# Token halves between the two layers of a hybrid attention kernel, with GpSimd adding residuals and summing squares

## The chip, the cores and the metric

One Trainium2 chip, of which the kernel uses one core. The metric is the time of one execution on the device, in microseconds (us). A core has five engines that run from queues of their own and wait for each other by semaphores: TensorE (PE in the profile; PEld is its weight load), VectorE (DVE), ScalarE (ACT), GpSimd (POOL) and SyncE (SP), which here only issues DMAs.

## The reference

Two layers are computed one after the other on 512 tokens of width 2048, in float32: a first layer with latent attention (MLA) and forgetting attention, and a second one with compressed, selected and windowed attention. What matters here lies between them:

```python
def _hybrid_layer(x, ...):
    ...
    o = jnp.concatenate([o_mla, o_fox], axis=-1) @ w_out
    return x + _rms_norm(o, g_post)

def second_block(x, w_in, ...):
    h = _rmsnorm(x, norm_g[l])
    proj = h @ w_in[l]
```

So the output projection `o` of the first layer needs its norm over all 2048 features, is scaled and added to `x`, and the sum needs a norm of its own before the second layer's projection. The second norm's factor per token can be applied after the projection, the first one's can't, since `x` is added in between.

## The kernel before

Activations lie transposed: 128 features on the partitions, 512 tokens along a row, 16 such tiles (`KT`) for 2048 features, in the array `o`. Each float32 product is made of three matmuls (`three`, line 419): a high part of the weights with a high part and with a rest of the activations, and the rest of the weights with the high part. `xh` and `xl` hold the two parts of the activations, `wh` and `wl` those of the weights.

Weights come in units of 128 x 1024 into four slots. SyncE loads a unit into `raw` once the slot's unit before it has been split; ScalarE copies the high part into `wh` (`act_hi`, line 973, which waits until TensorE has used the slot, `w_used`), and VectorE subtracts to get `wl` (`lo`, line 1429). A strip is 128 output features: two units, 16 x 3 matmuls of 512 columns.

The output projection of the first layer (`U_OUT1`) is 16 strips (`half`, line 440). VectorE evacuates each (`out1`, line 1898), ScalarE squares it into `e_t`, and VectorE adds the squares into `acc`. After the last strip:

- TensorE sums the columns of `acc` and `e_t` (`pe_token_sums`, line 548), so that each token's sum of squares lies on a partition.
- VectorE and ScalarE make the factor per token and lay it on diagonal matrices in `gate` (`token_rms`, line 1535; `act_root`, line 1018), and TensorE spreads it over all partitions with a matmul (`pe_spread`, line 560), into the PSUM bank `po`.
- TensorE runs six filler matmuls (`WARM_MID`, line 714).
- VectorE scales each tile by `g_post` and that bank (`scale_tile`, line 1923). Tiles 0 and 1 get `x` added by VectorE from `xr1` (`residual`, line 1928). For tiles 2 to 15 GpSimd issues a DMA that adds `x` from memory into the tile (line 389), at most four in flight, and it stores the sums to memory in four DMAs (line 383) for the end of the second layer.
- ScalarE makes `xh` and the squares of each tile (lines 1258 and 1261), VectorE makes `xl` (`x_rest`, line 1594) and adds the squares to `acc` (`square_in`, line 1602).
- TensorE runs four strips of the second projection at once, tile by tile (`pe_four`, line 517): 16 x 4 x 3 matmuls of 512 columns, and ahead of its last two tiles the sum of squares of the second norm (`pe_sum`, line 543).

The order of the work is written out by hand, engine by engine, and each queue is executed in order. At the very end of the kernel the same work is already done in token halves (`last_strip`, line 929), where GpSimd multiplies five tiles per half (line 416), and that stage is used below as a source of durations. It starts at about 1815 us.

## Time and profile before

| | us |
|---|---|
| median of 3 runs | 1853.12 |
| lowest and highest run | 1852.43, 1853.68 |
| the profiled execution, its own time | 1853.12 |
| its span, first to last instruction | 1851.4 |
| PE busy | 1823.4 (98%) |
| VectorE, ScalarE, GpSimd busy | 1047.4, 665.6, 36.3 |
| mean granted clock of TensorE | 0.994 of full speed |

The profile is of one execution. A line of it names an engine, a source line, what was written and from what, a count and times. Matmuls are pipelined, so the distance between the starts of two of them tells their cost, not the length of one record. On the other engines, too, an instruction can start a little before the end of the record before it. A row of the chain of waits is a start, a length and the engine and line on which the end of the kernel depended at that time.

### The profile page before, as it was taken

How to read it: one execution, taken by the hardware profiler on the slowest of the kernel's cores; microseconds unless marked ns; L12 is line 12 of the kernel's file. 1: busy time of each engine (PE TensorE's matmuls, PEld its weight loads, DVE VectorE, ACT ScalarE, POOL GpSimd, SP SyncE). 2: the span in 40 equal slices, each digit the busy share in tenths (PEclk: the TensorE clock that was granted, in tenths of full speed). 3: DMA queues.
4: the chain of work that ended last, by engine and by line, in shares of the span. 5: the costliest groups of instructions: out<-in, count | busy, mean ns of one | idle time of the engine just before them, and what ended most of it. 6: DMA issues, size and time to landing. Idle time of an engine off the chain costs nothing.

```text
span 1851.4 us, 25537 instructions
## 1 busy us (share of the span) xinstructions
PE 1823.4 (98%) x9060; PEld 1514.8 (82%) x9060; DVE 1047.4 (57%) x1768; ACT 665.6 (36%) x1279; POOL 36.3 (2%) x58
## 2 busy tenths in 40 slices
PE   9999999999999999999999999999999999999997
PEld 7788888888888887878868887888888888888887
DVE  7643434444433787853348954766767566665334
ACT  6532332322223544432226342433433333443222
POOL 0000000000000000000002000000000000000001
PEclk9999999999999999999999999999999999999998
DMA  6322222222232333232237363211112222124333
GB/s 237 106 86 91 79 79 91 86 84 82 89 102 80 126 114 113 91 112 93 91 101 218 102 227 124 70 57 57 68 57 69 92 68 79 66 70 136 115 115 102
DMA packets 56021, 186.16 MB, mean 101 GB/s; under 512 B 6688, under 2 KB 11168, under 8 KB 55456
## 3 DMA queue, kind: packets, MB, share of 16 engines
q1 hardware_dynamic: 51328, 170.78, 27.6%
q0 software_dynamic: 4640, 14.68, 3.0%
q8 instruction: 33, 0.54, 0.1%
q14 instruction: 20, 0.16, 0.0%
HBM read 177.05 MB, written 8.39 MB: 100 GB/s over the span
## 4 chain that ended last, share of the span: by engine, by line
PE 90%; DVE 5%; DVEq 2%; ACT 1%; issue 1%; POOL 0%; POOLq 0%; ACTq 0%
PE strip L421 23%; PE strip L423 22%; PE strip L422 22%; PE scores L421 4%; PE scores L422 3%; PE scores L423 3%; PE outputs L423 2%; PE outputs L422 2%; PE outputs L421 1%; PE scores L476 1%; PE scores L869 1%; PE scores L828 1%; PE scores L897 1%; DVE wl L1433 1%; DVEq L1438 0%
## 5 line engine op out<-in xcount | busy, mean ns | idle before, releaser
L421 PE MATMUL strip<-xh,wh 128*128 128x512 f32 (+1 forms) x1976 | 779.7, 395 | 5.7 <-DVE xl L1825 3.2
L423 PE MATMUL strip<-xh,wl 128*128 128x512 f32 (+1 forms) x1976 | 768.0, 389 | 0.0
L422 PE MATMUL strip<-xl,wh 128*128 128x512 f32 (+1 forms) x1976 | 767.2, 388 | 0.0
L421 PEld LDWEIGHTS strip<-xh,wh 128*128 128x128 f32 x1976 | 371.9, 188 | 82.4 <-DVE xl L1825 4.8
L423 PEld LDWEIGHTS strip<-xh,wl 128*128 128x128 f32 x1976 | 371.6, 188 | 77.3
L422 PEld LDWEIGHTS strip<-xl,wh 128*128 128x128 f32 x1976 | 372.3, 188 | 72.7 <-issue 0.7
L1433 DVE TENSOR_TENSOR wl<-raw,wh 128x1024 fp32r<-128x1024 f32 (+3 forms) x306 | 354.7, 1177 | 119.1 <-ACT wh L979 118.2
L979 ACT ACTIVATE wh<-raw 128x1024 fp32r<-128x1024 f32 (+3 forms) x308 | 306.9, 1023 | 109.7 <-PE strip L423 107.1
L1001 ACT ACTIVATE prob<-scores,nms 128x128 f32<-128x128 f32 (+3 forms) x128 | 65.9, 532 | 129.7 <-DVE nms L1481 129.7
L1241 ACT ACTIVATE e_t<-o 128x512 f32 (+1 forms) x30 | 19.0, 632 | 222.0 <-DVE o L1902 118.1
L421 PE MATMUL scores<-xh,wh 128*128 128x512 f32 (+1 forms) x240 | 91.6, 382 | 0.0
L423 PE MATMUL scores<-xh,wl 128*128 128x512 f32 (+1 forms) x240 | 90.1, 375 | 0.0
L422 PE MATMUL scores<-xl,wh 128*128 128x512 f32 (+1 forms) x240 | 90.0, 375 | 0.0
L1441 DVE TENSOR_TENSOR y<-strip,rb 128x512 f32<-128x512 f32 x45 | 31.1, 692 | 75.7 <-PE strip L423 73.1
L1479 DVE TENSOR_REDUCE nm<-scores 128x1 f32<-128x128 f32 (+1 forms) x96 | 41.2, 485 | 55.1 <-PE scores L457 54.3
L984 ACT ACTIVATE q_h<-y 128x512 fp32r<-128x512 f32 x24 | 15.2, 632 | 145.8 <-DVE y L1454 107.2
L994 ACT ACTIVATE e_t<-y 128x512 f32<-128x512 f32 x32 | 20.5, 641 | 127.4 <-DVE y L1441 127.4
L1505 DVE TENSOR_TENSOR ptl<-scores,pth 128x512 fp32r<-128x512 f32 (+3 forms) x128 | 53.8, 483 | 9.7 <-ACT pth L1009 9.6
L421 PEld LDWEIGHTS scores<-xh,wh 128*128 128x128 f32 x240 | 45.2, 188 | 9.0 <-issue 0.5
L422 PEld LDWEIGHTS scores<-xl,wh 128*128 128x128 f32 x240 | 45.2, 188 | 8.7 <-issue 0.7
L423 PEld LDWEIGHTS scores<-xh,wl 128*128 128x128 f32 x240 | 45.2, 188 | 8.1
L1902 DVE COPY o<-strip 128x512 f32 (+1 forms) x14 | 9.7, 692 | 74.0 <-PE strip L423 73.9
(426 smaller groups left out, 1875.6 us busy)
## 6 DMA issues: line engine op xcount, KB each, us to landing
raw<-in_w SPq DMA_DIRECT2D x308, 512.0 KB, 3.2
xn<-o POOLq DMA_DIRECT2D x4, 1024.0 KB, 7.8
xr<-xn POOLq DMA_DIRECT2D x16, 256.0 KB, 3.0
o<-in_xt SPq DMA_DIRECT2D x7, 512.0 KB, 7.9
o<-in_xt POOLq DMA_DIRECT2D x14, 256.0 KB, 6.3
out<-o SPq DMA_DIRECT2D x14, 256.0 KB, 2.7
raw<-in_w SPq DMA_DIRECT2D x2, 256.0 KB, 4.6
o<-in_xt SPq DMA_DIRECT2D x2, 256.0 KB, 5.1
```

What stands on the lines that cost most here:

```text
L421: pe.matmul(out, ah, bh, start=first, stop=False, skip_group_check=shared)
L422: pe.matmul(out, ah, bl, start=False, stop=False, skip_group_check=shared)
L423: return pe.matmul(out, al, bh, start=False, stop=last, skip_group_check=shared)
L476: ins = pe.transpose(sb[t][:, P * (w - t):P * (w - t) + P], prob[:, ROW[w] + P * t:ROW[w] + P * t + P], ident[:, :])
L979: a.activation(wh[s][:, :cols], raw[s][:, :cols], ACT.Copy).then_inc(w_hi, 1)
L994: a.activation(e_t[:, :], src, ACT.Tanh, scale=0.5).then_inc(ev_act, 1)
L1001: a.activation(prob[:, ROW[t]:ROW[t] + w], sb[t][:, pre[t]:pre[t] + w], ACT.Exp, bias=nms[:, t:t + 1], scale=scale, accum_out=lsum[:, t:t ...
L1241: a.activation(e_t[:, :], src, ACT.Square).then_inc(ev_act, 1)
L1433: v_.tensor_tensor(wl[s][:, :cols], raw[s][:, :cols], wh[s][:, :cols].bitcast(F32), ALU.subtract)\
L1441: v_.tensor_tensor(dst, src[:, :], times[:, :], ALU.mult).then_inc(y_done, 1)
L1479: v_.tensor_reduce(nm[:, t:t + 1], sb[t][:, 0:P * (t + 1)], AX.X, ALU.max, negate=True)
L1505: v_.tensor_tensor(ptl[:, cols], sb[t][:, 0:w], pth[:, cols].bitcast(F32), ALU.subtract)\
```

## The change

The last two strips of the first layer and the first six tiles (`HT = 6`) of the second projection are worked in two halves of 256 tokens. The sums, the factor and the spreading are done once for each half. GpSimd adds `x` to tiles 0 to 5 from `xr1`, which now holds six tiles and lies elsewhere in memory, half by half, and sums all squares of the second norm into a new array `acc_mid`; four buffers `sq` take the place of two. The additions into `acc_mid` wait for each other by the semaphore `sq_used`, with no drain between them. Tiles 6 to 15 still get `x` by accumulating DMAs. The filler matmuls are gone. Semaphore counts that the end of the kernel waits for are moved along; its work is the same.

The diff, cut to its core:

```diff
-WARM_FIRST, WARM_MID = 5, 6
+WARM_FIRST = 5
+HT = 6
+X_MID = 3 * KT - 6
+X_OUT2 = 4 * KT - 6 + HT
...
-    sq = [place("sq0", [P, S], offset=at["prob"] + 2048), place("sq1", [P, S], offset=at["prob"] + 4096)]
+    sq = [place("sq0", [P, S], offset=at["prob"] + 2048), place("sq1", [P, S], offset=at["prob"] + 4096),
+          place("sq2", [P, S], offset=at["pth"] + 2048), place("sq3", [P, S], offset=at["pth"] + 4096)]
+    acc_mid = place("acc_mid", [P, S], offset=at["pth"])
...
-    xr1 = place("xr1", [P, 2, S], offset=at["y"])
...
+    xr1 = place("xr1", [P, HT, S], offset=kv0)
...
+    def sq_part(hf, j):
+        n_ = HT * hf + j
+        return sq[n_ // 2 % 4][:, 256 * (n_ % 2):256 * (n_ % 2) + 256]
...
+        g.memset(acc_mid[:, :], 0.0).then_inc(blk_zero, 1)
+        g.dma_start(xr1[:, :, :], d["xt"][:, 0:HT, :]).then_inc(xr1_in, 16)
         g.dma_start(cos2[:, :], d["cos_a"]).then_inc(tab2_in, 16)
         g.dma_start(sin2[:, :], d["sin_a"]).then_inc(tab2_in, 16)
+        def residual(hf, j):
+            g.wait_ge(scaled, HT * hf + j + 1)
+            part = o[:, j, TOKENS[hf]]
+            g.tensor_tensor(part, part, xr1[:, j, TOKENS[hf]], ALU.add).then_inc(xn_done, 1)
...
+        def x_added_in(j):
+            if j - 4 >= HT:
+                x_is_added(j - 4)
+            g.wait_ge(scaled, HT + j + 1)
+            g.dma_start(o[:, j, :], d["xt"][:, j, :], accum_op=ALU.add).then_inc(x_added[j % 4], 16)
+        def square_half(hf, j):
+            if HT * hf + j:
+                g.wait_ge(sq_used, KT + HT * hf + j)
+            else:
+                g.wait_ge(blk_zero, 2)
+            g.wait_ge(sq_done, KT + HT * hf + j + 1)
+            g.tensor_tensor(acc_mid[:, TOKENS[hf]], acc_mid[:, TOKENS[hf]], sq_part(hf, j), ALU.add).then_inc(sq_used, 1)
+        def square(j):
+            g.wait_ge(sq_used, KT + HT + j)
+            g.wait_ge(sq_done, KT + HT + j + 1)
+            g.tensor_tensor(acc_mid[:, :], acc_mid[:, :], sq[j % 4][:, :], ALU.add).then_inc(sq_used, 1)
...
-        for j in range(2, KT):
-            if j >= 6:
-                x_is_added(j - 4)
-            g.wait_ge(scaled, j - 1)
-            g.dma_start(o[:, j, :], d["xt"][:, j, :], accum_op=ALU.add).then_inc(x_added[j % 4], 16)
-            if j == 7:
-                g.wait_ge(xn_done, 2)
-            if j in (7, 11, 15):
-                xn_store(j - 7)
+        g.wait_ge(xr1_in, 16)
+        for j in range(HT):
+            residual(0, j)
+            if j >= 3:
+                square_half(0, j - 3)
+        residual(1, 0)
+        square_half(0, 3)
+        residual(1, 1)
+        square_half(0, 4)
+        residual(1, 2)
+        x_added_in(6)
+        residual(1, 3)
+        x_added_in(7)
+        residual(1, 4)
+        square_half(0, 5)
+        residual(1, 5)
+        x_added_in(8)
+        square_half(1, 0)
+        x_added_in(9)
+        for j in range(1, HT):
+            square_half(1, j)
+        g.wait_ge(xn_done, 2 * HT)
+        xn_store(0)
+        for j in range(HT, KT):
+            if j + 4 < KT:
+                x_added_in(j + 4)
+            if j == 8:
+                xn_store(4)
+            if j == 12:
+                xn_store(8)
+            square(j)
...
+    def pe_mid(pe, u0, outs, aside):
+        def tile(j, s, tokens, first, last):
+            slot = (u0 + j // 2) % SLOTS
+            cols = slice(512 * (j % 2) + P * s, 512 * (j % 2) + P * s + P)
+            return three(pe, outs[s][:, tokens], wh[slot][:, cols], wl[slot][:, cols], xh[:, j, tokens],
+                         xl[:, j, tokens], first, last, shared=True)
+        for hf in range(2):
+            for j in range(HT):
+                pe.wait_ge(x_lo, X_MID + HT * hf + j + 1)
+                if hf == 0 and j % 2 == 0:
+                    pe.wait_ge(w_lo, u0 + j // 2 + 1)
+                for s in range(4):
+                    ins = tile(j, s, TOKENS[hf], hf == 0 and j == 0, False)
+                if hf == 1 and j % 2 == 1:
+                    ins.then_inc(w_used, 1)
+                if hf == 0:
+                    aside(j)
+        for u in range(HT // 2, 8):
+            if u == 7:
+                pe.wait_ge(sq_used, KT + HT + KT)
+                pe.matmul(px[:, :], ones[:, :], acc_mid[:, :], start=True, stop=True).then_inc(sum_done, 1)
+            steps = [(2 * u + a, s) for a in range(2) for s in range(4)]
+            if u == 7:
+                steps = [(2 * u + a, s) for s in range(4) for a in range(2)]
+            for j, s in steps:
+                if s == 0:
+                    pe.wait_ge(x_lo, X_MID + HT + j + 1)
+                    pe.wait_ge(w_lo, u0 + u + 1)
+                ins = tile(j, s, slice(0, S), False, j == KT - 1)
+                if j == KT - 1 and s < 3:
+                    ins.then_inc(four_done, 1)
+            ins.then_inc(w_used, 1)
...
-        pe_token_sums(pe, 3, N_OUT1 + KT)
-        pe_spread(pe, 0, (po,))
-        for i in range(WARM_MID):
-            pe.matmul(px[:, :], ones[:, :], gate[:, :], start=True, stop=True)
-        pe_four(pe, U_CMPIN, 3 * KT - 6, sb, summed=(4, 7))
+        def out1_half(hf, j, steps):
+            if steps[0] == 0:
+                if hf == 0:
+                    pe.wait_ge(y_done, N_OUT1 + 13 + j)
+                else:
+                    pe.wait_ge(half_out, j + 1)
+            pe_half_strip(pe, U_CMPIN - 4 + 2 * j, pj[(N_OUT1 + j) % 2], hf, steps)
+        out1_half(0, 0, range(KT))
+        out1_half(0, 1, range(KT))
+        out1_half(1, 0, range(5))
+        pe_half_sums(pe, 0, 4, (half_sq, 2))
+        out1_half(1, 0, range(5, KT))
+        pe.wait_ge(diag_done, 2)
+        pe.matmul(po[:, 0:256], ones[:, :], gate[:, 0:256], start=True, stop=True).then_inc(spread, 1)
+        out1_half(1, 1, range(KT))
+        def aside(j):
+            if j == 1:
+                pe_half_sums(pe, 1, 5, (ev_act, N_OUT1 + KT))
+            if j == 3:
+                pe.wait_ge(diag_done, NQ)
+                pe.matmul(px[:, :], ones[:, :], gate[:, :], start=True, stop=True).then_inc(spread, 1)
+        pe_mid(pe, U_CMPIN, sb, aside)
...
+        def sq_half(hf, j):
+            if HT * hf + j >= 8:
+                a.wait_ge(sq_used, KT + HT * hf + j - 7)
+            a.activation(sq_part(hf, j), o[:, j, TOKENS[hf]], ACT.Square).then_inc(sq_done, 1)
+        half_square(0, 0)
+        half_square(0, 1)
+        act_root(a, 3, 0, 2)
+        half_square(1, 0)
+        act_hi(a, At(U_CMPIN))
+        xh_half(0, 0)
+        xh_half(0, 1)
+        act_hi(a, At(U_CMPIN + 1))
+        xh_half(0, 2)
+        for j in range(3):
+            sq_half(0, j)
+        xh_half(0, 3)
+        half_square(1, 1)
         act_hi(a, At(U_CMPIN + 2))
+        xh_half(0, 4)
+        sq_half(0, 3)
+        xh_half(0, 5)
+        act_root(a, 4, 2, 4)
         act_hi(a, At(U_CMPIN + 3))
-        act_root(a, 3)
-        for j in range(KT):
-            if j < 2:
-                a.wait_ge(xn_done, j + 1)
-            else:
-                a.wait_ge(x_added[j % 4], 16 * (j // 4 + (j % 4 >= 2)))
+        for j in (4, 5):
+            sq_half(0, j)
+        for j in range(HT):
+            xh_half(1, j)
+            if j in (3, 5):
+                act_hi(a, At(U_CMPIN + (j + 5) // 2))
+            sq_half(1, j)
+        for j in range(HT, KT):
+            a.wait_ge(x_added[j % 4], 16 * ((j - HT) // 4 + 1))
             a.activation(xh[:, j, :], o[:, j, :], ACT.Copy, scale=c("g_2", j)).then_inc(x_hi, 1)
-            if j >= 2:
-                a.wait_ge(sq_used, KT + j - 1)
-            a.activation(sq[j % 2][:, :], o[:, j, :], ACT.Square).then_inc(sq_done, 1)
-            if j in (5, 7, 9, 11):
-                act_hi(a, At(U_CMPIN + (j + 3) // 2))
+            a.wait_ge(sq_used, KT + 2 * j - 6 if j < 9 else KT + HT + j - 3)
+            a.activation(sq[j % 4][:, :], o[:, j, :], ACT.Square).then_inc(sq_done, 1)
+            if j in (8, 10):
+                act_hi(a, At(U_CMPIN + j // 2 + 2))
         act_hi(a, At(U_CMPIN + 8))
-        act_rms(a, 4)
+        act_rms(a, 5)
...
+        def out1_half(hf, j):
+            if hf == 0:
+                v_.wait_ge(part_done, j + 1)
+            else:
+                v_.wait_ge(w_used, U_CMPIN - 2 + 2 * j)
+            v_.tensor_copy(o[:, 14 + j, TOKENS[hf]], pj[(N_OUT1 + j) % 2][:, 0:256])\
+              .then_inc(half_out if hf == 0 else y_done, 1)
+        def half_add(hf):
+            v_.drain()
+            if hf == 0:
+                v_.wait_ge(half_sq, 1)
+            else:
+                v_.wait_ge(ev_act, N_OUT1 + 15)
+            v_.tensor_tensor(acc[:, TOKENS[hf]], acc[:, TOKENS[hf]], e_t[:, TOKENS[hf]], ALU.add)
+            v_.drain().then_inc(acc_ready, 1)
+        def scale_half(hf, j):
+            factor = (po[:, 0:256], px[:, 256:512])[hf]
+            v_.scalar_tensor_tensor(o[:, j, TOKENS[hf]], o[:, j, TOKENS[hf]], c("g_post", j), factor, ALU.mult, ALU.mult)\
+              .then_inc(scaled, 1)
+        def rest_half(hf, j):
+            v_.wait_ge(x_hi, X_MID + HT * hf + j + 1)
+            v_.scalar_tensor_tensor(xl[:, j, TOKENS[hf]], o[:, j, TOKENS[hf]], c("g_2", j),
+                                    xh[:, j, TOKENS[hf]].bitcast(F32), ALU.mult, ALU.subtract).then_inc(x_lo, 1)
+        def scale_tile(j):
+            v_.scalar_tensor_tensor(o[:, j, :], o[:, j, :], c("g_post", j), px[:, :], ALU.mult, ALU.mult).then_inc(scaled, 1)
         for j in range(2):
             out1(0, 0)(j, U_OUT1 + 3 + j)
         two_strips(At(U_OUT1 + 4), out1(2, 0, banks=sb[0:2]))
         with v_.Fori(1, KT // 2 - 2) as i:
             two_strips(At(U_OUT1 + 4, i, 4), out1(2, i))
-        two_strips(At(U_CMPIN - 4), out1(14, 0, True))
-        token_rms(v_, 3)
-        v_.memset(acc[:, :], 0.0)
+        for j in range(2):
+            lo(v_, At(U_CMPIN - 2 + j))
+        out1_half(0, 0)
+        half_add(0)
+        out1_half(0, 1)
+        token_rms(v_, 3, 0, 2)
+        out1_half(1, 0)
+        v_.wait_ge(spread, 1)
+        scale_half(0, 0)
+        scale_half(0, 1)
+        half_add(1)
+        v_.drain().then_inc(r_done, 1)
+        scale_half(0, 2)
+        lo(v_, At(U_CMPIN))
+        rest_half(0, 0)
+        rest_half(0, 1)
+        scale_half(0, 3)
+        lo(v_, At(U_CMPIN + 1))
+        rest_half(0, 2)
+        out1_half(1, 1)
+        v_.drain().then_inc(r_done, 1)
+        scale_half(0, 4)
+        scale_half(0, 5)
+        rest_half(0, 3)
         lo(v_, At(U_CMPIN + 2))
+        rest_half(0, 4)
+        token_rms(v_, 4, 2, 4)
+        rest_half(0, 5)
         lo(v_, At(U_CMPIN + 3))
-        v_.wait_ge(spread, 1)
-        def scale_tile(j):
-            ins = v_.scalar_tensor_tensor(o[:, j, :], o[:, j, :], c("g_post", j), po[:, :], ALU.mult, ALU.mult)
-            if j >= 2:
-                ins.then_inc(scaled, 1)
-        def residual(j):
-            v_.drain()
-            v_.tensor_tensor(o[:, j, :], o[:, j, :], xr1[:, j, :], ALU.add).then_inc(xn_done, 1)
-        scale_tile(0)
-        v_.wait_ge(xr1_in, 16)
-        residual(0)
-        scale_tile(2)
-        scale_tile(1)
-        x_rest(0, o[:, 0, :], c("g_2", 0), 3 * KT - 6)
-        residual(1)
-        scale_tile(3)
-        for j in range(KT):
+        v_.wait_ge(spread, 2)
+        for j in range(3):
+            scale_half(1, j)
+        rest_half(1, 0)
+        scale_half(1, 3)
+        rest_half(1, 1)
+        scale_half(1, 4)
+        rest_half(1, 2)
+        scale_half(1, 5)
+        scale_tile(6)
+        rest_half(1, 3)
+        scale_tile(7)
+        rest_half(1, 4)
+        rest_half(1, 5)
+        lo(v_, At(U_CMPIN + 4))
+        scale_tile(8)
+        scale_tile(9)
+        for j in range(HT, KT):
+            x_rest(j, o[:, j, :], c("g_2", j), X_MID + HT)
             if j + 4 < KT:
                 scale_tile(j + 4)
-            if j:
-                x_rest(j, o[:, j, :], c("g_2", j), 3 * KT - 6)
-            if j:
-                square_in(j - 1, KT)
-            if j in (5, 7, 9, 11):
-                lo(v_, At(U_CMPIN + (j + 3) // 2))
-        square_in(KT - 1, KT)
-        v_.drain().then_inc(acc_ready, 1)
+            if j in (6, 8, 10):
+                lo(v_, At(U_CMPIN + j // 2 + 2))
         lo(v_, At(U_CMPIN + 8))
-        rms_ms(v_, 4, D)
-        rms_rb(v_, 4, rb)
+        rms_ms(v_, 5, D)
+        rms_rb(v_, 5, rb)
```

## Rows read from the trace of the kernel before

**Rows 1.** The page: busy time of each engine
```profile
PE 1823.4 (98%) x9060; PEld 1514.8 (82%) x9060; DVE 1047.4 (57%) x1768; ACT 665.6 (36%) x1279; POOL 36.3 (2%) x58
```

**Rows 2.** Chain of waits, 955 to 970 us (start, us, what)
```profile
955.37 0.24 PE strip L423
...
961.01 2.07 PE outputs L564 x2
963.08 6.84 PE odds L715 x12
969.92 0.23 PE scores L421
```

**Rows 3.** Busy time by stretch: engines, granted clock, DMA share, GB/s
```profile
963.00:967.00 4.00, 4.00 (x7) 1.64 (x6) 3.93 (x6) 1.24 (x2) 0.90 (x1) 0.58 0.69 211
```

**Rows 4.** The timeline of PE: weight strips, 512 columns (start, us, what)
```profile
949.99 0.39 PE L421 MATMUL strip<-xh,wh 128*128 128x512 f32 x1
950.22 0.39 PE L422 MATMUL strip<-xl,wh 128*128 128x512 f32 x1
```

**Rows 5.** The timeline of PE in the last stage: 256 columns and column sums
```profile
1820.07 0.28 PE L422 MATMUL strip<-xl,wh 128*128 128x256 f32 x1
1820.19 0.28 PE L423 MATMUL strip<-xh,wl 128*128 128x256 f32 x1
...
1827.15 0.50 PE L948 MATMUL odds<-ones,acc 128*128 128x1 f32 x4
...
1827.96 0.36 PE L421 MATMUL scores<-xh,wh 128*128 128x256 f32 x1
```

**Rows 6.** The chain of waits, the sum of squares at 1008 us
```profile
1008.04 0.86 PE odds L546 x2
```

**Rows 7.** The timeline of VectorE in the last stage
```profile
1821.42 0.43 DVE L2257 TENSOR_TENSOR acc<-acc,e_t 128x256 f32<-128x256 f32 x1 [2.22 <-ACT e_t L1423]
...
1828.13 0.16 DVE L1539 TENSOR_SCALAR nm<-odds 128x2 f32<-128x2 f32 x1 [3.17 <-PE odds L952]
...
1829.52 0.48 DVE L1550 TENSOR_SCALAR gate<-ident,rinv 128x128 f32<-128x128 f32 x2
...
1832.27 0.83 DVE L2257 TENSOR_TENSOR acc<-acc,e_t 128x256 f32<-128x256 f32 x1 [0.73 <-ACT e_t L1423]
1833.23 4.40 DVE L2242 SCALAR_TENSOR_TENSOR o<-o,cvec,outputs 128x256 f32<-128x256 f32 x11
```

**Rows 8.** The timeline of GpSimd in the last stage; one addition, two, then five
```profile
1832.08 0.73 POOL L416 TENSOR_TENSOR o<-o,rb 128x256 f32<-128x256 f32 x1 [17.06 <-ACT rb L1426]
...
1832.78 0.91 POOL L416 TENSOR_TENSOR o<-o,rb 128x256 f32<-128x256 f32 x1
...
1843.60 3.45 POOL L416 TENSOR_TENSOR o<-o,rb 128x256 f32<-128x256 f32 x5 [7.82 <-ACT rb L1426]
```

**Rows 9.** Groups of VectorE, 955 to 1006 us (busy us, mean ns, idle before)
```profile
L1599 DVE SCALAR_TENSOR_TENSOR xl<-o,cvec,xh 128x512 fp32r<-128x512 f32 x16 | 12.0, 747 | 0.3 <-ACT xh L1258 0.3
L1924 DVE SCALAR_TENSOR_TENSOR o<-o,cvec,outputs 128x512 f32<-128x512 f32 x16 | 11.6, 742 | 0.0
...
L1433 DVE TENSOR_TENSOR wl<-raw,wh 128x1024 fp32r<-128x1024 f32 x7 | 8.4, 1212 | 0.1
```

**Rows 10.** ScalarE, 256-column squares: durations ns min/median/max, first and last start
```profile
L1423 ACT ACTIVATE e_t<-o x4: 401/412/419, 1821.0 to 1838.0; 128x256 f32<-128x256 f32 x4
```

**Rows 11.** GpSimd: two DMA issues; length and landing of the accumulating ones
```profile
974.61 0.87 POOL L389 DMA_DIRECT2D o<-in_xt  x1 [1.24 <-DVE o L1924]
975.15 0.89 POOL L383 DMA_DIRECT2D xn<-o  x1
...
DMA to landing us min/median/max: 4.2/6.3/8.9
```

**Rows 12.** Line 416, GpSimd: durations ns min/median/max, first and last start
```profile
L416 POOL TENSOR_TENSOR o<-o,rb x10: 722/730/914, 1832.1 to 1846.3; 128x256 f32<-128x256 f32 x10
L416 POOLq MODIFY_POOL_CONFIG  x2: 37/37/37, 1815.0 to 1815.0; - x2
```

97 lines of the change are left out of this document (53 added, 44 removed).

## The prediction

> **What bounds the kernel now.** I read the page first, for what fills the span: TensorE (PE) is busy 98% of 1851.4 us, the others far less [rows 1]. So a change is worth only what it does to TensorE's stream. I then followed the chain of waits to where that stream carries no work of the reference. Between the layers the last weight strip's matmul ends at 955.61 (955.37 + 0.24), and the first matmul of the second layer's projection stands at 969.92 [rows 2]. The 14.3 us between them hold the column sums, the wait for the rms, the spreading matmul and 12 records of filler matmuls (6.84 us), which keep the clock up while VectorE, ScalarE and a DMA prepare the first tile. The granted clock fell all the same: 0.58 in 963 to 967 us, which is the lower level, 1.2 GHz [rows 3]. From 969.92 on TensorE stays dense.
>
> **The gap goes, and what TensorE does instead.** Strips 14 and 15 are cut into two token halves, so the rms, the scaling and the first projection tiles of tokens 0 to 255 are prepared while tokens 256 to 511 are still being multiplied.
> - Removed: 14.3 us.
> - Halves are dearer: a 512-column matmul comes every 0.227 us [rows 4], a 256-column one every 0.120 us, not 0.1134 [rows 5]. The change issues 192 of them for the strips and 2 x 6 x 4 x 3 = 144 for the first six projection tiles: 336 x 0.0066 = 2.2 us.
> - Column sums twice, 0.81 us each (1827.15 to 1827.96) [rows 5]: 1.6. Spreads: one of 512 columns at the 0.86 us of the sum of squares [rows 6], one of 256 at half of that: 1.3. The sum of squares at 1008 us stays.
>
> Net without a single wait: 14.3 - 2.2 - 1.6 - 1.3 = 9.2 us gained. Nearly all of it hangs on the helpers keeping up.
>
> **The helpers' durations.** VectorE, 256 columns with the factor in PSUM: 11 in 4.40 us, 0.40 apart, 0.475 long; an addition from SBUF 0.43; nm to the gate tiles 1828.13 to 1830.00, 1.87 [rows 7]. GpSimd, 256 columns: 0.73 alone, five in 3.45, so 0.68 to 0.70 apart [rows 8]. A 512-column addition on GpSimd is in no row: at least 0.73, at most two halves, 1.46; I take 1.30, nearer the upper end, since its fixed part is paid once. The rest tiles take 0.75, scaling 512 columns 0.74, the low part of a weight unit 1.21 [rows 9]. ScalarE needs 0.41 for 256 columns [rows 10]; its copy with a scale I take at 0.5. GpSimd issues two DMAs 0.54 apart, each 0.87 long, and an accumulating one lands after 4.2 to 8.9 us [rows 11]; an addition behind an issue starts 0.54 to 0.87 after it. A chained addition waits for the one before to end: 0.73 + 0.1 instead of 0.70; only the squares are chained, and the 10 late ones matter, 1 us in all, inside the 1.30 to 1.46. The configuration for GpSimd's additions ran at 1815.0, 17 us ahead of its first addition and unseen by it [rows 12]; now it comes with the early DMAs near 803 us: nothing.
>
> **Stretch A, up to the second spread.** The half strips start at 933.8 (955.6 less two strips of 10.9). 192 x 0.12 + 0.8 + 0.4 puts the first projection tile at 958.1, and four half tiles of 1.44 and the second column sums put TensorE at the second spread at 964.7. VectorE has, from the first spread at 952.5: 6 scalings (2.4), one addition (0.5), 3 weight lows at 1.14 apart (3.4), 5 half rests (2.0), a copy (0.4), the rms (1.9), 0.5 of waits: 963.6. Hidden, with 1 us of cover. Weight slots come free as each half-1 strip passes, 2 us ahead.
>
> **Stretch B, half 1 of tiles 0 to 5, and tile 6.** From the spread to the first rest: scale 0.5, GpSimd 0.9, ScalarE 0.55, rest 0.5, about as long as the two half tiles TensorE still has. Then GpSimd's written order bites. It issues the accumulating DMA of tile 6 ahead of the residual of tile 3, and that DMA waits for the scaling of tile 6, which VectorE does behind the rest of tile 2. From residual 2 to residual 3: 0.73 + 0.05 + 0.5 + 0.05 + 0.4 + 0.4 + 0.74 + 0.15 + 0.54 = 3.6 us, where TensorE eats a half tile in 1.44. Tile 7's DMA does the same ahead of residual 4: 3.2. Tile 6's own rest stands behind a weight low and two scalings (2.5). With 0.4 us of slack: stalls of 1.8, 1.7 and 1.7, together 5.2 us.
>
> **Stretch C, tiles 7 to 15.** TensorE wants the sum of squares 21.8 us after it starts tile 6 (8 x 2.72). GpSimd by then has 5 chained half squares (4.0), 10 full ones (13.0) and 11 DMA issues (5.9 to 9.6): 22.9 to 26.6. The last square comes about 1 us late, and tiles 8 and 10, whose data land late, cost 1.2: 2.2 us.
>
> So far: 9.2 - 5.2 - 2.2 = 1.8 us gained.
>
> **The new collision.** One place of the trace shows GpSimd adding beside a VectorE instruction that reads two SBUF tensors. The addition of line 2257 took 0.43 us at 1821.42, alone, and 0.83 at 1832.27, where GpSimd's addition had begun at 1832.08 [rows 7]. GpSimd's next one, 1832.78, took 0.91 where the others take 0.73 [rows 8]. So each waited for the other: 0.40 us on VectorE, 0.18 on GpSimd, though in 1843.60 to 1847.05, where VectorE's second operand lies in PSUM, five additions ran freely. This is one meeting, but the change makes dozens: 24 half and 10 full additions on GpSimd against 22 rests, 9 weight lows and one addition on VectorE, all reading two SBUF tensors.
> - A: about 6 meetings x 0.40 on VectorE = 2.4, less 1 of cover: TensorE waits 1.4 at the second spread.
> - B: each link of the chain is longer by a meeting; 1.3 more.
> - C: GpSimd has no slack left, and 10 squares of double width are each held up by a rest or a low, 2 x 0.18 = 0.36 each: 3.6 more. Upper issue spacing: 0.9 more.
>
> The Trainium skill (SBUF — State Buffer, "SBUF: two separate sides") states this as a rule: a VectorE instruction with two SBUF inputs and a reading GpSimd instruction exclude each other, the later one fully blocked. The trace agrees in kind, but not in full: blocked to the end of GpSimd's 0.73 us, the addition would have ended at 1833.24, and it ended at 1833.10. The same skill's GPSIMD Engine Reference (§3.1) gives about 2.6 cycles an element at 1.2 GHz, an estimate of 1.28 us for the unseen 512-column addition; the sum by it is the same.
>
> **Sum.** 1.8 - 1.4 - 1.3 - 3.6 - 0.9 = -5.4 us: slower. The profiled execution took 1853.12, equal to the median of the runs, for a span of 1851.4; so 1858.5 us. Bounds of this case: meetings at half their price and the lower issue spacing, 2.4 slower; additions of 1.46, landings of 6.8 and the higher prices, 9.9 slower: 1855.5 to 1863.0.
>
> **Rivals.** About 0.2%, 3.7 us, is what a measurement of this kernel can tell from no change.
> - Full exclusion: every meeting serial, GpSimd's 30 us of additions and VectorE's 24 us of two-input work in one line from 953 us. That is 54 us, so the last square ends at 1007 at best and, with the idle turns between, near 1013 to 1018; the projection ends 10 us later than now: 1863. For it the 0.40 us; against it that GpSimd lost only 0.18. The rule of the Trainium skill named above is this case.
> - No collision to speak of: the one meeting was an accident of dispatch. Then 1.8 gained, -1 to +4 by landing time: 1851.3.
> - Faster: GpSimd's order costs nothing because the scalings run ahead of my count, the stalls of B and C are under 3 us in all, and the gap's 9.2 us are kept to two thirds: 1847. It decides at tile 3 of half 1: if its rest is done within 1.5 us of tile 2's, this is the case. For it: VectorE and ScalarE have idle time between those tiles by my count. Against: the DMA of tile 6 stands ahead in GpSimd's queue whatever they do.
>
> **Chances.** The forecast 0.55 (0.42 slower by over 0.2%, 0.13 within), full exclusion 0.12 (slower), no collision 0.18 (0.13 within, 0.05 faster), stalls hidden 0.15 (faster). Faster 0.20, same 0.26, slower 0.54. The range 1850.5 to 1864.0 leaves out most of the last rival and the far end of full exclusion. The likeliest case's own range is 1855.5 to 1863.0.
>
> **What would show it.** No filler and no gap near 955; first projection tile 24 us after the half strips start; the second spread 1 to 2 us late; waits of TensorE on rest tiles 3, 4 and 6, each released by VectorE behind ScalarE behind GpSimd; VectorE's half rests at 0.8 to 1.0 us where they meet an addition, GpSimd's halves at 0.9 and more; the sum of squares waiting for GpSimd. Wrong if the rests keep 0.43 us beside GpSimd's additions, if a 512-column addition is far from 1.3 us, or if TensorE stands idle long enough for its clock to fall to the lower level, which would add to the loss.

## The result, and the profile after

The changed kernel takes 1864.87 us (median of 4 runs, 1863.67 to 1865.09), the kernel before 1853.40 (4 runs beside it): a ratio of 1.0061, 95% interval 1.0049 to 1.0073. It is slower, by 11.5 us (0.6%, and the interval leaves out no change), where 5.4 were forecast and 1864.0 was the end of the range.

First the page of the kernel after, to set against [rows 1]: its span, and busy time by engine.

```profile
span 1863.4 us, 25891 instructions
PE 1824.2 (98%) x9218; PEld 1522.3 (82%) x9218; DVE 1049.9 (56%) x1769; ACT 668.2 (36%) x1294; POOL 70.7 (4%) x89
```

TensorE (PE) is busy about as long as before, in a span 12.0 us longer: what is new is idle time. GpSimd (POOL) has gone from 36.3 us to 70.7. Next, what TensorE waited for between 930 and 1040 us: the timeline of the matmuls behind its waits (start, us, operation, and in brackets the idle time before it and what ended it). Two waits of 0.24 and 0.27, at tiles 7 and 9, are left out.

```profile
967.41 1.12 PE L836 MATMUL odds<-gate,ones 128*128 128x512 f32 x2 [1.31 <-DVE gate L1704]
978.62 0.39 PE L477 MATMUL scores<-xh,wh 128*128 128x256 f32 x1 [2.41 <-DVE xl L2084]
982.87 0.38 PE L477 MATMUL scores<-xh,wh 128*128 128x256 f32 x1 [2.55 <-DVE xl L2084]
987.92 0.51 PE L477 MATMUL scores<-xh,wh 128*128 128x512 f32 x1 [0.78 <-DVE xl L1753]
...
1004.33 0.50 PE L477 MATMUL scores<-xh,wh 128*128 128x512 f32 x1 [4.07 <-DVE xl L1753]
1019.11 1.12 PE L652 MATMUL odds<-acc_mid,ones 128*128 128x512 f32 x2 [2.00 <-POOL acc_mid L414]
```

The gap of [rows 2] is gone. In its place stand waits at the second spread (stretch A), at tiles 3 and 4 of the second half and at tile 6 (B), at tile 10 and at the sum of squares (C). Windows of after, with the columns of [rows 3] (the granted clock stands third from the end):

```profile
985.00:990.00 5.00, 4.22 (x20) 3.57 (x19) 5.00 (x6) 1.70 (x3) 4.25 (x5) 0.72 0.79 177
1000.00:1005.00 5.00, 0.93 (x5) 0.59 (x4) 1.42 (x3) 2.23 (x4) 3.59 (x4) 0.99 1.06 232
1005.00:1010.00 5.00, 5.00 (x17) 3.92 (x16) 4.54 (x4) 2.85 (x5) 2.76 (x3) 0.67 1.05 295
```

So the granted clock, too, falls twice, behind the waits of tile 4 and of tile 10; the means of 0.72 and 0.67 mix full speed with the lower level, 1.2 GHz. Now GpSimd, whose timeline answers to [rows 8] and [rows 11] (L401 and L417 issue DMAs, L392 adds a residual half, L409 half squares, L414 full ones):

```profile
975.83 0.92 POOL L401 DMA_DIRECT2D o<-in_xt  x1 [2.42 <-DVE o L2088]
976.44 1.06 POOL L392 TENSOR_TENSOR o<-o,xr 128x256 f32<-128x256 f32 x1
979.53 0.90 POOL L401 DMA_DIRECT2D o<-in_xt  x1 [2.02 <-DVE o L2088]
980.15 1.03 POOL L392 TENSOR_TENSOR o<-o,xr 128x256 f32<-128x256 f32 x1
...
987.57 6.33 POOL L409 TENSOR_TENSOR acc_mid<-acc_mid,sq 128x256 f32<-128x256 f32 x5
993.83 0.60 POOL L417 DMA_DIRECT2D xn<-o  x1
994.43 0.89 POOL L401 DMA_DIRECT2D o<-in_xt  x1
995.00 1.63 POOL L414 TENSOR_TENSOR acc_mid<-acc_mid,sq 128x512 f32<-128x512 f32 x1
...
1005.48 0.87 POOL L401 DMA_DIRECT2D o<-in_xt  x1 [1.89 <-DVE o L2088]
...
1009.42 0.86 POOL L401 DMA_DIRECT2D o<-in_xt  x1 [1.76 <-DVE o L2088]
```

Twice, at 975.83 and 979.53, a DMA issue waits for a scaling on VectorE with a residual behind it: stretch B as forecast. Then five half squares run in a row, and the DMA of tile 10 comes behind them and behind a store of 1 MB, at 994.43, although VectorE had finished that tile's scaling (L2088) at 988.5 by its own timeline. The transfer then took 8.3 us to land, where the middle of the ten took 5.4. First the scaling, then the landing of all ten and of tile 10's alone:

```profile
987.79 0.73 DVE L2088 SCALAR_TENSOR_TENSOR o<-o,cvec,odds 128x512 f32<-128x512 f32 x1
...
DMA to landing us min/median/max: 4.3/5.4/8.7
...
DMA to landing us min/median/max: 8.3/8.3/8.3
```

Last the groups of both engines in 935 to 1030 us (count, busy us, mean ns, idle before), for [rows 8, 9].

```profile
L414 POOL TENSOR_TENSOR acc_mid<-acc_mid,sq 128x512 f32<-128x512 f32 x10 | 17.7, 1770 | 0.2
L409 POOL TENSOR_TENSOR acc_mid<-acc_mid,sq 128x256 f32<-128x256 f32 x12 | 12.3, 1024 | 0.3
L1753 DVE SCALAR_TENSOR_TENSOR xl<-o,cvec,xh 128x512 fp32r<-128x512 f32 x10 | 14.8, 1490 | 6.7 <-ACT xh L1413 6.7
```

A full rest tile on VectorE takes 1.49 us on average, where it took 0.75.

**A measure for the runs.** The stage goes from the first half strip (934.96 in after; 933.8 in before by the forecast's working) to the first strip matmul behind the projection (1025.54; 1014.22). I split its length by windows into TensorE's idle time, its busy time times (1 - granted clock), and the rest; the split is good to some 0.2 us. The stages are of single profiled executions, and the times beside them medians of the timed runs, so a stage and a median do not always move alike: the profiled executions of order_a and set_after were the slowest of theirs (1861.65 and 1862.90), those of vsq and vsq2 the fastest (1849.55 and 1849.41).

| kernel | stage us | idle | lower clock | rest | time, ratio to before (95%) |
|---|---|---|---|---|---|
| before | 80.4 | 3.6 | 2.7 | 74.1 | 1853.40 |
| after | 90.6 | 13.6 | 3.2 | 73.8 | 1864.87, 1.0061 (1.0049 to 1.0073) |
| order_a | 86.8 | 10.3 | 3.2 | 73.3 | 1858.73, 1.0028 (1.0018 to 1.0039) |
| order_b | 88.3 | 11.3 | 3.7 | 73.4 | 1859.86, 1.0038 (1.0024 to 1.0053) |
| x10_first | 83.4 | 6.9 | 3.4 | 73.0 | 1855.91, 1.0011 (1.0001 to 1.0020) |
| store_late | 83.7 | 8.6 | 1.7 | 73.5 | 1857.43, 1.0023 (1.0012 to 1.0034) |
| no_sq | 79.5 | 5.0 | 1.7 | 72.9 | 1854.67, 1.0009 (0.9999 to 1.0018) |
| set_after | 88.6 | 9.9 | 5.5 | 73.2 | 1861.74, 1.0040 (1.0026 to 1.0053) |
| fill | 90.5 | 10.0 | 0.0 | 80.5 | 1865.61, 1.0064 (1.0050 to 1.0078) |
| vsq | 78.7 | 4.8 | 0.0 | 73.9 | 1851.72, 0.9988 (0.9979 to 0.9997) |
| vsq2 | 77.9 | 4.0 | 0.0 | 73.9 | 1850.23, 0.9984 (0.9975 to 0.9993) |

The stage holds 10.2 of the 12.0 us between the two spans. Another 0.7 lie behind it, and 1.1 before it: both kernels wait some 2.3 us for VectorE at 770 us, in code the change does not touch, and behind it the clock was at the lower level in the profiled execution of after and not in that of before. It was down there in 8 of the 16 profiles of this study other than micro's, so I take this for chance and no part of the change. First before, then after:

```profile
773.00:775.00 2.00, 2.00 (x9) 1.61 (x10) 1.83 (x6) 2.00 (x4) 0.00 (x0) 1.00 0.00 0
```

```profile
773.00:775.00 2.00, 2.00 (x6) 1.61 (x5) 1.83 (x7) 2.00 (x4) 0.00 (x0) 0.50 0.00 0
```

### The profile page after: what moved, and what is told of

It is laid out like the page before. It is cut to its first block, busy times and chain, and to the rows that moved or that the text cites. A ratio compares the mean times of both kernels' runs of the same rounds, so it can differ in the third digit from the quotient of the medians.

```text
span 1863.4 us, 25891 instructions
## 1 busy us (share of the span) xinstructions
PE 1824.2 (98%) x9218; PEld 1522.3 (82%) x9218; DVE 1049.9 (56%) x1769; ACT 668.2 (36%) x1294; POOL 70.7 (4%) x89
## 4 chain that ended last, share of the span: by engine, by line
PE 85%; DVE 6%; POOL 2%; issue 2%; DVEq 2%; ACT 2%; DMA 0%; POOLq 0%; ACTq 0%
PE strip L477 22%; PE strip L479 22%; PE strip L478 22%; PE scores L477 3%; PE scores L478 3%; PE scores L479 3%; PE outputs L479 2%; PE outputs L478 2%; PE outputs L477 1%; PE scores L532 1%; DVE wl L1587 1%; PE scores L991 1%; PE scores L950 1%; PE scores L1019 1%; POOL acc_mid L409 1%
## 5 line engine op out<-in xcount | busy, mean ns | idle before, releaser
L477 PEld LDWEIGHTS strip<-xh,wh 128*128 128x128 f32 x2008 | 378.2, 188 | 81.7 <-DVE xl L1979 4.8
L479 PEld LDWEIGHTS strip<-xh,wl 128*128 128x128 f32 x2008 | 378.1, 188 | 76.8
L478 PEld LDWEIGHTS strip<-xl,wh 128*128 128x128 f32 x2008 | 378.4, 188 | 72.0 <-issue 0.7
L477 PE MATMUL scores<-xh,wh 128*128 128x512 f32 (+1 forms) x264 | 97.8, 370 | 10.3 <-DVE xl L1753 5.4
L478 PEld LDWEIGHTS scores<-xl,wh 128*128 128x128 f32 x264 | 50.8, 192 | 7.6 <-issue 0.5
L479 PEld LDWEIGHTS scores<-xh,wl 128*128 128x128 f32 x264 | 50.7, 192 | 7.5
L1123 ACT ACTIVATE pth<-scores 128x512 fp32r<-128x512 f32 (+3 forms) x128 | 45.0, 437 | 12.3 <-PE scores L950 9.7
```

The costliest lines, as they stand in the source:

```text
L477: pe.matmul(out, ah, bh, start=first, stop=False, skip_group_check=shared)
L478: pe.matmul(out, ah, bl, start=False, stop=False, skip_group_check=shared)
L479: return pe.matmul(out, al, bh, start=False, stop=last, skip_group_check=shared)
L1123: a.activation(pth[:, COL[t]:COL[t] + w], sb[t][:, 0:w], ACT.Copy).then_inc(pt_hi, 1)
```

## Experiments

**The durations by themselves.** A small kernel with sections parted by barriers: `v.tensor_tensor` x12 and `g.tensor_tensor` x6, alone and side by side.

> The disputed durations by themselves. This kernel leaves out the whole computation and writes zeros; its sections, parted by barriers, hold 12 VectorE instructions of 512 columns and 6 GpSimd ones, first each alone, then side by side. Theory 1 (the collision is a property of two SBUF inputs on VectorE beside any GpSimd addition): alone VectorE 0.75 us, GpSimd 0.73 for 256 columns and 1.3 to 1.6 for 512; side by side each VectorE instruction that meets an addition takes 0.4 us and more longer, and GpSimd's 0.2; with VectorE's second operand in PSUM, and beside GpSimd's memset, nothing changes. Rival (GpSimd's 512-column addition is simply that slow, 1.6 us, and chaining adds 0.2): GpSimd 1.56 alone and 1.79 apart when chained alone, and little changes side by side. Full exclusion: side by side the two engines' times add up, 12 x 0.67 + 6 x 1.4 or more = 16 us and over for the section, against some 9 for the longer engine alone.

The timeline of its sections (start, us, what, count). Alone: VectorE 512 columns, GpSimd 256, 512, and 512 chained by a semaphore. Then side by side: 512 on both, and 512 with VectorE's second operand in PSUM; last VectorE beside memsets and beside accumulating DMAs.

```profile
6.42 7.32 DVE L65 TENSOR_TENSOR vout<-vin 128x512 f32<-128x512 f32 x12 [2.35 <-POOLq L105]
13.85 4.12 POOL L110 TENSOR_TENSOR gout<-gin 128x256 f32<-128x256 f32 x6 [12.16 <-DVEq L60]
18.14 7.35 POOL L113 TENSOR_TENSOR gout<-gin 128x512 f32<-128x512 f32 x6 [0.18 <-DVEq L60]
...
26.25 7.96 POOL L118 TENSOR_TENSOR gacc<-gacc,gin 128x512 f32<-128x512 f32 x6
34.32 13.71 DVE L75 TENSOR_TENSOR vout<-vin 128x512 f32<-128x512 f32 x12 [20.59 <-POOLq L105]
34.41 10.06 POOL L122 TENSOR_TENSOR gout<-gin 128x512 f32<-128x512 f32 x6 [0.20 <-POOL gacc L118]
...
55.58 7.26 DVE L83 TENSOR_TENSOR vout<-vin,bank 128x512 f32<-128x512 f32 x12
...
76.89 7.32 DVE L91 TENSOR_TENSOR vout<-vin 128x512 f32<-128x512 f32 x12
84.33 7.32 DVE L95 TENSOR_TENSOR vout<-vin 128x512 f32<-128x512 f32 x12
```

A 512-column addition comes every 0.61 us on VectorE (7.32 / 12), and on GpSimd every 1.22 us alone (7.35 / 6) and 1.33 chained (7.96 / 6). Side by side VectorE loses 13.71 - 7.32 = 6.4 us to six additions, 1.07 for each of 1.22, and GpSimd loses 0.45 for each. That is close to full exclusion: six of VectorE's instructions (3.7 us) and all of GpSimd's (7.35) fit into 10.06 us. In this small kernel it takes two SBUF inputs on VectorE and an addition, which reads SBUF, on GpSimd: with VectorE's second operand in PSUM, or a memset or accumulating DMAs on GpSimd's side, VectorE keeps 7.3. The rule of the Trainium skill (SBUF — State Buffer, "SBUF: two separate sides") says the same, that the later instruction fully blocks and that a GpSimd instruction which only writes does not count; this run agrees, but for 0.15 us of each addition.

**GpSimd's order in stretch B.** The residuals ahead of the DMAs.

```
         residual(1, 2)
-        x_added_in(6)
         residual(1, 3)
-        x_added_in(7)
         residual(1, 4)
-        square_half(0, 5)
         residual(1, 5)
+        x_added_in(6)
+        x_added_in(7)
+        square_half(0, 5)
         x_added_in(8)
```

> Only GpSimd's written order is changed, by putting the residuals of tiles 3 to 5 of the second half ahead of the accumulating DMAs of tiles 6 and 7. Queue-order theory: the waits of 2.41, 2.55 and 0.78 us before tiles 3 to 5 and the clock's fall behind them (1.1) go, and nothing inherits them: 6 us less than after, 1859. Rival (the squares are the bound of stretch C): tile 10's transfer stays behind GpSimd's burst of half squares, TensorE comes to it earlier and waits longer, 4 us becomes 8 or more: 1863 to 1865, same as after. In between if part of the wait is passed on.

The median fell by 6.1 us, to 1858.73; the stage of the profiled execution, the slowest of its eight, is 3.8 us shorter. All waits of TensorE in the stage:

```profile
967.60 1.12 PE L836 MATMUL odds<-gate,ones 128*128 128x512 f32 x2 [1.33 <-DVE gate L1704]
983.47 0.50 PE L477 MATMUL scores<-xh,wh 128*128 128x512 f32 x1 [2.58 <-DVE xl L1753]
1000.73 0.50 PE L477 MATMUL scores<-xh,wh 128*128 128x512 f32 x1 [4.45 <-DVE xl L1753]
1015.52 1.12 PE L652 MATMUL odds<-acc_mid,ones 128*128 128x512 f32 x2 [1.97 <-POOL acc_mid L414]
```

The waits of tiles 3 and 4 are gone (the one of 0.78 was tile 6's, not tile 5's as I had written). Tile 6's wait has grown to 2.58, so the expectation that nothing inherits them failed. Tile 10 and the sum wait about as before: the rival, that C takes the gain back, is out.

**And in stretch C.** On top of order_a, the DMAs of tiles 10 to 12 between the half squares, the later ones ahead of full squares, the stores later (their lines are left out here).

```
         square_half(1, 2)
+        x_added_in(10)
...
         square_half(1, 4)
+        x_added_in(11)
         square_half(1, 5)
+        x_added_in(12)
         for j in range(HT, KT):
-            if j + 4 < KT:
-                x_added_in(j + 4)
+            if j + 7 < KT:
+                x_added_in(j + 7)
```

> As order_a, and the accumulating DMAs of tiles 10 to 12 stand between the half squares, the stores of the normalised input come three tiles later. If order on GpSimd's queue is all that cost the time: no wait over 1 us on tiles 3 to 15, the sum of squares 1 to 2 us late, 1855 to 1857. If GpSimd's load (its additions 1.3 to 2.0 us long beside VectorE) is the bound: the tiles come in time but the sum of squares comes 4 us late and more, 1858 to 1860. If collisions alone set it, no order helps: 1863 and more.

1859.86, so neither: tile 10 no longer waits and tile 11 only 0.60, but the wait before the sum rose to 6.68. I took that for GpSimd's load. It was in good part again an order: tiles 13 to 15 have their issues ahead of squares that were ready (half_v, below, shows it). Moving tile 10's DMA alone, on top of order_a:

```
         x_added_in(9)
-        for j in range(1, HT):
+        square_half(1, 1)
+        square_half(1, 2)
+        x_added_in(10)
+        for j in range(3, HT):
             square_half(1, j)
...
-            if j + 4 < KT:
+            if HT < j and j + 4 < KT:
                 x_added_in(j + 4)
```

> The kernel order_a (whole computation) with the accumulating DMA of tile 10 alone put ahead of GpSimd's last three half squares; the store of 1 MB stays where it was. If the half squares ahead of the issue make tile 10 late: it is issued some 3.5 us earlier, the wait of 4.45 us before it falls to 1.5 or less; what of it comes back at the sum of squares (1.97 in order_a) tells how far GpSimd's load binds: all of it back, 1858.5; none, 1855.5. If the store beside it makes it late, the wait stays over 3 us.

1855.91, 2.8 us under order_a. Tile 10 does not wait any more, tile 11, whose DMA still stands behind the half squares, does; and the wait before the sum fell with them:

```profile
1001.64 0.57 PE L480 MATMUL scores<-xh,wh 128*128 128x512 f32 x1 [2.76 <-DVE xl L1756]
1011.96 1.12 PE L655 MATMUL odds<-acc_mid,ones 128*128 128x512 f32 x2 [0.26 <-POOL acc_mid L414]
```

So GpSimd was not the bound by its load: it had been waiting for VectorE, which waited for a transfer that GpSimd had issued late. But the move also took tile 10's DMA out from behind the store, so it does not part the two. The store's part, also on top of order_a:

```
-        g.wait_ge(xn_done, 2 * HT)
-        xn_store(0)
         for j in range(HT, KT):
             if j + 4 < KT:
                 x_added_in(j + 4)
             if j == 8:
+                g.wait_ge(xn_done, 2 * HT)
+                xn_store(0)
+            if j == 11:
                 xn_store(4)
-            if j == 12:
+            if j == 13:
                 xn_store(8)
```

> The kernel order_a (whole computation) with the 1 MB store of tiles 0 to 3 moved from ahead of tile 10's DMA to behind the issue for tile 12, and the next two stores moved later with it. If the store's traffic makes tile 10's transfer land late (8.3 us in after, median 5.4): the wait of 4.45 us before tile 10 falls by 2 to 3 us. If the half squares ahead of the issue do it: it falls by the 0.5 us of the issue at most, 1858 to 1859, as order_a.

Tile 10 now waits 0.83 instead of 4.45, more than the 2 to 3 us that the expectation gave the store's traffic. Its DMA was issued at 987.37, 54.1 us into the stage, where order_a had 54.7: hardly earlier. But it landed in half the time. Its landing in order_a, in store_late and in x10_first, where it also stands ahead of the store:

```profile
DMA to landing us min/median/max: 9.3/9.3/9.3
...
DMA to landing us min/median/max: 4.5/4.5/4.5
...
DMA to landing us min/median/max: 6.9/6.9/6.9
```

So the store beside the transfer makes tile 10 late as much as the squares ahead of it do, and either move alone takes most of the wait away. What is gained there is in part lost again: tile 11 waits 1.37 and the sum 2.44 (1.97 in order_a), and now the stores run beside the last transfers, one of which took 9.2 us. The stage is 83.7 us, as long as x10_first's 83.4; the time is 1857.43, 1.3 under order_a, with intervals that overlap.

**The squares, left out.** The sum of squares is a constant in this kernel, so it does not compute the result.

```
-            if j >= 3:
-                square_half(0, j - 3)
...
-            square(j)
...
-                pe.wait_ge(sq_used, KT + HT + KT)
+                pe.wait_ge(sq_done, KT + HT + KT)
```

> GpSimd's written order as in after, but its 22 additions of squares are left out (the sum of squares of the second norm is a constant instead, so this part of the computation is missing); residuals, DMAs and stores stay. What the squares cost beside everything else: if the squares and their meetings with VectorE hold the loss, tile 10's wait (4.1), the wait at the sum (2.0), the second spread's wait (1.3) and the clock's second fall (1.8) go, and only the waits of tiles 3 to 5 with their fall stay: 1855 to 1857. If the order is at fault alone: the waits of tiles 3 to 5 stay, and tile 10 goes too, 1857 to 1859. If neither, 1863.

1854.67: the squares on GpSimd as a whole cost 10.2 of after's 11.5 us. Tiles 3 and 4 still wait, 1.19 and 1.98, by the order of residuals and DMAs, with the residuals' own meetings still in it.

**The squares, without their reads.** Each addition replaced by chained memsets, first in order_b, then in after; the sum is again a constant. The edit for a full square:

```
-            g.tensor_tensor(acc_mid[:, :], acc_mid[:, :], sq[j % 4][:, :], ALU.add).then_inc(sq_used, 1)
+            for i in range(2):
+                g.memset(acc_mid[:, 256 * i:512], 16.0).then_inc(setm, 1)
+                g.wait_ge(setm, sets + i + 1)
+            g.memset(acc_mid[:, :], 16.0).then_inc(sq_used, 1)
```

> The kernel order_b with each of GpSimd's additions of squares replaced by chained memsets of about the length that such an addition has alone (three of 256 and 512 columns in place of a full one, some 1.4 us; two in place of a half one, some 0.8), which read nothing; the sum of squares is a constant, so that part of the computation is missing. Shared-access theory (additions and VectorE's two-operand instructions lengthen each other): VectorE's 512-column rests fall from 1.02 us mean to 0.75 and the weight lows from 1.39 to 1.2, GpSimd's residuals keep some of theirs, its squares' places take 1.4, the wait before the sum falls from 6.7 us to 3 or less, and the time to 1855 to 1856. Load theory (GpSimd simply has too much to do in sequence): the wait before the sum stays at 5 us or more and the time at 1858 or more.

> The kernel after, in its own written order, with each of GpSimd's additions of squares replaced by chained memsets of about the length that such an addition has alone (some 1.5 us for a full one, 0.8 to 0.9 for a half one), which read nothing; the sum of squares is a constant, so that part of the computation is missing. no_sq showed that the squares as a whole cost after 10 us. Collision theory: these 10 us are the meetings of the two engines, so with the reads gone the time falls to 1857 or less. Load theory: they are GpSimd's hours in sequence, so the time stays at 1861 to 1864: the waits before tiles 3, 4 and 10 and before the sum stay, each shorter by a few tenths, and only VectorE's rests are back at 0.75 us.

set_sq took 1860.11, as order_b; its rests were back at 0.75 us and its wait before the sum stayed at 7.02. set_after took 1861.74, 3.1 us under after. Its rests, its two long waits, and the memsets that stand for one full square:

```profile
L1761 DVE SCALAR_TENSOR_TENSOR xl<-o,cvec,xh 128x512 fp32r<-128x512 f32 x10 | 7.5, 749 | 13.3 <-ACT xh L1421 13.3
```

```profile
978.48 0.39 PE L485 MATMUL scores<-xh,wh 128*128 128x256 f32 x1 [2.40 <-DVE xl L2092]
...
1003.98 0.79 PE L485 MATMUL scores<-xh,wh 128*128 128x512 f32 x1 [4.98 <-DVE xl L1761]
```

```profile
1012.13 0.90 POOL L420 MEMSET acc_mid<- 128x512 f32 x2
...
1013.67 0.90 POOL L420 MEMSET acc_mid<- 128x512 f32 x2
```

With every meeting of a square and a VectorE instruction gone, VectorE simply sits idle for longer ahead of its full rests, 13.3 us where it was 6.7. The reads explain at least 3 us of the 10, and the places of the squares in the queue at most 7. It is no sharper than that: the memsets of a full square come 1.54 us apart (1012.13 to 1013.67), where a chained addition alone takes 1.33, and behind tile 10 the granted clock was 0.50 from 1004 to 1009 us, ahead of a sum for which TensorE then waited for nobody.

**The clock.** Fillers into TensorE's waits.

```
+        def warm(n):
+            pe.wait_ge(scaled, HT)
+            for i in range(n):
+                pe.matmul(po[:, :], ones[:, :], gate[:, :], start=True, stop=True)
...
+                if hf == 1 and j in (3, 4):
+                    warm(2)
...
+                    if j == 10:
+                        warm(3)
```

> The kernel after (whole computation) with filler matmuls on TensorE, written to a bank that is free by then, in its three long waits: two ahead of tiles 3 and 4 of the second half and three ahead of tile 10, at 1.08 us each by the spread's two passes in the trace of vsq2, so each group a little shorter than its wait. Clock theory: after lost 3.2 us in this stage to a clock at the lower level (its windows: 0.5 after the wait of tile 4 and after that of tile 10); with TensorE busy instead, the clock stays up and 2.5 to 3 us come back: 1862, a mean of 2 us under after at least. Rival: the waits themselves decide and the lost clock is made up in them, because what TensorE waits for comes no earlier: 1864 to 1865, as after.

The clock stayed at 1.00 through the stage, and nothing came back: 1865.61, the stage 90.5 us against 90.6. TensorE reached its next waits earlier and waited longer there (1.92 where it was 0.78):

```profile
989.16 0.50 PE L477 MATMUL scores<-xh,wh 128*128 128x512 f32 x1 [1.92 <-DVE xl L1762]
```

In this kernel the helpers set the time from the second spread to the sum, and a slower TensorE costs nothing there. My theory of 3 us for the clock falls.

**The squares on VectorE.** GpSimd keeps residuals, DMAs and stores in order_b's order.

```
+        def square(j):
+            v_.drain()
+            v_.wait_ge(sq_done, KT + HT + j + 1)
+            v_.tensor_tensor(acc_mid[:, :], acc_mid[:, :], sq[j % 4][:, :], ALU.add).then_inc(sq_used, 1)
...
         rest_half(1, 0)
         scale_half(1, 3)
+        square_half(0, 0)
         rest_half(1, 1)
```

> The whole computation, with the 22 additions of squares on VectorE (12 of 256 columns at about 0.45 us and 10 of 512 at about 0.72, 12.6 us in all, each behind a drain) and only residuals, accumulating DMAs and stores on GpSimd, in the order of order_b. If GpSimd's share of the squares is what costs the time, and VectorE has room for 12.6 us in 60: no wait over 1 us behind the second spread, the sum of squares 0 to 1 us late, the stage 3 to 4 us shorter than no_sq's: 1850 to 1853, at or under the kernel before. If VectorE becomes the bound (its rests come late by what the squares in front of them take): waits of 0.5 to 1 us on most tiles of the second half and on tiles 6 to 9, 1855 to 1859.

vsq is faster than both kernels: 1851.72, though against before only by 0.12% (its interval ends at 0.9997). Its successors, each with the core of its edit:

```
+        scale_tile(6)
         rest_half(1, 2)
         scale_half(1, 5)
...
+                if j == KT - 1 and s == 0:
+                    pe.wait_ge(sq_used, KT + HT + KT)
```

> The kernel vsq (whole computation) with two of its remaining waits attacked: tile 6 is scaled two places earlier on VectorE and its accumulating DMA is issued ahead of the residual of tile 5 (the wait of 1.32 us before tile 6), and TensorE's sum of squares stands six matmuls later, behind the first strip's last tiles (the wait of 1.41 us). If these waits bound the stage: 1.5 to 2.5 us less than vsq, 1849 to 1850.5. If VectorE, which vsq's trace shows without a pause from 966 to 1006 us, is the bound, the waits come back on the neighbours: 1851 to 1852, as vsq.

```
+        def res_half(hf, j):
+            part = o[:, j, TOKENS[hf]]
+            v_.tensor_tensor(part, part, xr1[:, j, TOKENS[hf]], ALU.add).then_inc(xn_done, 1)
```

> The kernel vsq (whole computation) with the 12 half residual additions on VectorE too, so that GpSimd only issues DMAs. VectorE does 12 x 0.35 = 4.2 us more and some drains, is rid of every meeting (its half rests 0.63 us mean in vsq against 0.475 alone, weight lows 1.26 against 1.22, first scalings slower too: some 3 us), and each tile's way has one engine less. If VectorE's time is the bound: equal to vsq within 1.5 us, 1851 to 1853.5. If the way over a second engine was the bound: the second spread's wait of 0.79 and the half tiles' waits of 0.7 go, 1850. Worse, 1855, if the drains and the denser queue push all of stretch B back.

```
-        lo(v_, At(U_CMPIN + 2))
         rest_half(0, 4)
         token_rms(v_, 4, 2, 4)
+        lo(v_, At(U_CMPIN + 2))
...
         rest_half(1, 5)
+        x_rest(HT, o[:, HT, :], c("g_2", HT), X_MID + HT)
```

> The kernel vsq2 (whole computation) with three turns of VectorE's written order: the low part of weight unit 2 behind the second rms instead of ahead of it, the rest of tile 6 ahead of two scalings and two squares, and the low parts of units 5 to 7 one tile later. If the order on VectorE is what is left: the waits of 0.80 (second spread), 1.31 (tile 6) and 0.47 (tile 7) go and the stage takes 75.5 us instead of 77.9: 1848. If VectorE's sum of work is the bound, what is moved comes late elsewhere (tile 8 or 9, or a weight unit): 1850, as vsq2.

vsq2, which scales tile 6 earlier and puts TensorE's sum later, brings 1850.23, 14.6 us under after and 3 under before: the sum's wait went (0.20), tile 6's did not (1.31). vres, with the residuals on VectorE too: 1851.63, as vsq; an engine less on the residuals' way is worth nothing, and VectorE does them at no loss. vsq3, a turn of VectorE's order: 1852.23, ratio 0.9991 (0.9982 to 1.0000), its stage 78.2 us, so no better: the waits of the spread and of tile 6 went and came back as 0.60 and 0.55 at half tiles, and 1.33 and 0.47 at tiles 7 and 8. That fits the rival, that VectorE's sum of work is what is left; it is not shown apart from other orders.

**Half of it, and one part alone.** half_v: the 12 half squares on VectorE, the 10 full ones on GpSimd. before_gsq: the kernel before, its 16 squares moved to GpSimd.

```
-            if j:
-                square_in(j - 1, KT)
...
+            if j >= 5:
+                square(j - 5)
```

> Between order_b and vsq (whole computation): the 12 half squares are added by VectorE, the 10 full ones by GpSimd. If GpSimd's late load of full squares binds (10 at 1.6 to 1.8 us and 6 issues and 4 stores, some 22 us behind the last half square, which VectorE adds near 988.5): the sum comes at 1011, 4 us late, 1856 to 1857. If the half squares were the burden, because they keep GpSimd from its issues: no wait over 1.5 us, 1852.

> One part of the change alone: the kernel before, whole tiles and all, with its 16 additions of squares between the layers moved from VectorE to GpSimd, chained by a semaphore (whole computation). VectorE is rid of 16 x 0.61 = 9.8 us. From the sections measured alone and side by side, a 512-column addition on GpSimd takes 1.33 us chained and 1.7 beside VectorE and costs VectorE up to 1.07. If GpSimd's load is the bound wherever it stands: 14 DMA issues x 0.54 and 16 x 1.7 = 35 us from 969 us on end near 1008, just when TensorE wants the sum: 0 to 3 us slower than before. If the meetings are what costs: VectorE's rests come late to TensorE's tiles, with waits on many tiles, 3 us slower or more. If VectorE was relieved in earnest: no change, since before has no waits there.

half_v: 1859.94 (1.0034, 1.0022 to 1.0046), as order_b, and slower than either expectation. Its GpSimd:

```profile
991.66 0.86 POOL L401 DMA_DIRECT2D o<-in_xt  x1 [2.64 <-DVE o L2084]
992.23 1.62 POOL L414 TENSOR_TENSOR acc_mid<-acc_mid,sq 128x512 f32<-128x512 f32 x1
...
998.97 0.88 POOL L401 DMA_DIRECT2D o<-in_xt  x1 [2.96 <-DVE o L2084]
```

The last half square ends at 988.6 on VectorE, but the first full one starts at 992.23, and the third is held up until 999.58: each time an issue stands ahead that waits for a scaling. The squares were ready: ScalarE had written the first of them at 981.1 and filled the fourth buffer at 989.3, and then stood 3.93 us, until GpSimd freed one, ahead of the next tile's `xh`. So the order turns back on itself: the later issue waits for VectorE, VectorE for ScalarE, and ScalarE waited for an addition that the earlier issue had held up.

```profile
993.88 0.63 ACT L1411 ACTIVATE sq<-o 128x512 f32<-128x512 f32 x1 [3.93 <-POOL acc_mid L414]
```

The two delays make most of the 6.64 us before the sum. More buffers were not tried.

before_gsq: 1860.78 (1.0033, 1.0020 to 1.0046), slower than before. TensorE now waits 2.6 us in all for rests and 2.5 us for the sum, where before had neither:

```profile
L386 POOL TENSOR_TENSOR acc<-acc,sq 128x512 f32<-128x512 f32 x16 | 29.2, 1824 | 0.4
L1610 DVE SCALAR_TENSOR_TENSOR xl<-o,cvec,xh 128x512 fp32r<-128x512 f32 x16 | 23.3, 1468 | 0.8 <-ACT xh L1269 0.6
```

VectorE was spared 16 x 0.61 = 9.8 us and lost 23.3 - 12.0 = 11.3 on the rests alone [rows 9]: here the meetings do cost, since VectorE was nearly full (busy for 33.5 of the 36 us from 970 to 1006 in before). GpSimd's own lateness has a part too, the wait for the sum.

## Why the prediction was wrong in size

- **Direction, and the gap.** Right: slower, the gap gone, the first projection tile 24.3 us after the half strips (959.3).
- **Net without a wait, 9.2 us.** Too much: vsq2's stage without its idle time is 73.9 us, with no clock lost, so the net is 80.4 - 73.9 = 6.5. The second spread takes 1.1 us instead of 0.86, the sum of squares as much, and each of vsq2's eight waits costs TensorE some 0.27 us beyond its idle time: that is counted from the end of a record 0.39 long, where the next matmul would have started after 0.23, and the second matmul behind a wait comes 0.34 after the first. Together 2.7 us.
- **Stretch A, 1.4.** The number is right, 1.31, the reason only in part: no_sq, vsq and set_after still wait 0.8, so at most 0.5 of it was the squares' meetings, where all of it was put down to meetings.
- **Stretch B, 5.2 and 1.3.** Right in place, tiles 3, 4 and 6: 2.41 + 2.55 + 0.78 = 5.7 in all. Right in cause for tiles 3 and 4, shown by order_a, which takes their waits away, and by no_sq, where 1.19 and 1.98 stay without a single square. Tile 6's wait was forecast from its rest's place behind a weight low and scalings on VectorE; order_a does not take it away but makes it 2.58, and vsq3, which moves that rest forward, takes away the 1.31 of vsq2.
- **Stretch C: the step that failed.** "The last square comes about 1 us late, and tiles 8 and 10, whose data land late, cost 1.2: 2.2 us." I counted GpSimd's work, 22.9 to 26.6 us, and let tile 10 be late by its landing only. Its DMA is behind five half squares (6.33 us, where 4.0 were counted) and the store, so it was issued 5.9 us after its scaling; and beside the store's traffic it took 8.3 us to land, where 6.8 was the most that the bounds allowed. The wait is 4.07, and then tiles 14 and 15 are scaled late, so that GpSimd waits 1.89 and 1.76 for VectorE and the sum comes late. x10_first shows this loop: one DMA moved, 2.8 us. store_late shows the store's share: tile 10's wait falls from 4.45 to 0.83.
- **A 512-column addition, 1.30 us.** Right: 1.22 alone, 1.33 chained; 1.77 in after, where 1.30 + 0.36 were counted.
- **The collision.** 0.40 for VectorE was the price of a half addition; a full one costs 1.07. Its total, 1.4 + 1.3 + 3.6 = 6.3, stands against at least 3.1 (set_after); how far it was too high is not shown. Much of the blocked time fell on a VectorE that would have waited anyway. The no-collision rival, at 1851.3, is refuted twice: the small kernel shows the collision, and set_after, at 1861.7, shows that most of the waits did not need it.
- **The sum.** By TensorE's account: waits were forecast at 14.6 us in all (1.4 + 6.5 + 6.7) and came to 13.6; the net was 2.7 short, and 3.2 went to a slower clock: -6.5 + 13.6 + 3.2 = 10.3, for 10.2 measured. That the waits of stretch C come to 6.6 us, for 6.7 forecast, is luck: they stand elsewhere and for another reason, and they would be longer had TensorE not been slower on the way to them. For fill shows that neither a filler nor the clock moves the end, so the size is that of the helpers' chain. From the second spread (966.1 forecast, 967.41 less the 1.1 of chance measured) it was to reach tile 6 at 985.0 (0.9 for the spread, eight half tiles of 1.44 and 6.5 of waits) and the sum at 1013.5 (21.8 and 6.7 later); less the same 1.1, it reached them at 986.8 and 1018.0. So it was 1.6 us too short in B and 2.7 more in C. These two, 0.2 in A, 0.3 for the longer sum, the 1.1 of chance and 0.7 behind the stage are the 6.6 us between 5.4 and 12.0. The clock was a danger of the forecast's last sentence, and cost nothing in after.
- **The lower bound.** By its own terms (the meetings' 6.3 halved, 0.9 left out) it comes out at 1.4 us slower, not 2.4. The result lies beyond the other end.
- **The rivals.** Full exclusion named 1863 and came nearest in time, and the small kernel bears out its rule almost fully. But its mechanism, all additions and two-input instructions in one line, was not what bound: set_after has none of it for the squares and takes 1861.7. "Stalls hidden" was to be decided at tile 3 of the second half, by a rest within 1.5 us of tile 2's: they are 4.1 us apart (973.98 and 978.08), so it is out.

Open: how much of stretch B's 1.6 us is the meetings of residuals and rests, which no run took away alone with the squares in place; how much of tile 10's lateness each of the two causes would keep without the other in after itself; the 0.7 us behind the stage; and why the clock falls behind the same idle time in some executions only.

## What to carry to other kernels

An engine's in-order queue that mixes waits on another engine with work others need is priced by its order, not by its load: for each entry ask what stands ahead of it, whom that waits for, and what traffic runs beside it. Here two moves in one queue were worth 9 of 11.5 us, and a store put later brought a transfer in after 4.5 us instead of 9.3. And moving a 512-column addition of two SBUF operands from VectorE to GpSimd spares a busy VectorE 0.61 us and can cost it 1.07; the best kernel found kept the token halves and gave the squares back to VectorE.

## What the hardware showed that was not expected

The collision is wider than one row had shown, 1.07 of a 512-column addition's 1.22 us, and in micro it vanishes with a memset, accumulating DMAs or a PSUM operand on one side. A 1 MB store beside an accumulating DMA of 256 KB went with 8.3 to 9.3 us of landing instead of 4.5. And the same idle time of 2.3 us of TensorE, in code that all these kernels share, was followed by the lower clock, 1.2 GHz, in eight profiled executions (granted clock 0.50 in 773 to 775 us of after) and not in eight others (1.00 in before); the half strips started from 934.3 us on in the eight and by 934.0 in the others.
